# Attention in-projection as three fp32r products per block, and expert outputs added to token rows in DRAM by an accumulating indirect DMA

## What is computed

```python
def moba_mixer(h, pos, k_past, v_past, w_in, w_out):
    proj = (h @ w_in).astype(jnp.float32)
    q, k, v = jnp.split(proj, [nqd, nqd + nkd], axis=-1)
    ...
def moe_swiglu(h, w_router, w_gate, w_up, w_down):
    logits = (h @ w_router).astype(jnp.float32)
    top_val, top_idx = lax.top_k(logits, TOP_K)
    wts = jax.nn.softmax(top_val, axis=-1)
    gates = jnp.sum(jax.nn.one_hot(top_idx, N_EXPERTS) * wts[..., None], axis=-2)
    y = jnp.zeros(h.shape, jnp.float32)
    for e in range(N_EXPERTS):
        y = y + gates[..., e:e + 1] * swiglu(h, w_gate[e], w_up[e], w_down[e])
    return y
```

## Time and profile before

| | us |
|---|---|
| runs of the kernel before | 1921.21, 1921.53, 1923.94 (median 1921.53) |
| the profiled execution, its own time | 1925.23 |
| its span from first to last instruction | 1923.0 |
| TensorE busy | 1779.1 (93%) |
| VectorE busy | 1293.0 (67%) |
| ScalarE busy | 968.4 (50%) |
| in-projection of attention | 606 to 675 |
| K and V pages read | 678 to 832 |
| router and gather of the first expert | 873 to 909 |
| experts | 909 to 1897 |

### The profile page before, as it was taken

How to read it: one execution, slowest core, us unless ns; L and a number is a source line. 1 busy time by engine, 2 the same in 40 slices (tenths; PEclk the granted TensorE clock), 3 DMA queues, 4 the chain that set the end, 5 groups by cost and what they waited for, 6 DMA issues and landing times.

```text
span 1923.0 us, 26967 instructions
## 1 busy us (share of the span) xinstructions
PE 1779.1 (93%) x9794; PEld 1483.7 (77%) x9794; DVE 1293.0 (67%) x1399; ACT 968.4 (50%) x908; POOL 53.3 (3%) x82
## 2 busy tenths in 40 slices
PE   5999988899999973896999999999999999999996
PEld 4888886899997731365888888888888888888885
DVE  5864573555543241014888888988889888888885
ACT  3442230444431030002777777776777777777773
POOL 1240000000000000000000000000000000000000
PEclk9998798999999996885999999999999999999998
DMA  7322123355546699972899999999999999999991
GB/s 291 110 80 103 48 118 154 138 190 177 178 157 238 201 325 386 346 300 89 317 363 384 346 370 362 345 382 350 365 365 334 387 352 362 371 348 358 357 351 57
DMA packets 98893, 521.85 MB, mean 271 GB/s; under 512 B 11066, under 2 KB 11259, under 8 KB 46067
## 3 DMA queue, kind: packets, MB, share of 16 engines
q1 hardware_dynamic: 82592, 482.72, 66.8%
q10 hardware_dynamic: 13970, 25.46, 3.7%
q0 software_dynamic: 2240, 12.49, 1.8%
HBM read 512.30 MB, written 8.33 MB: 271 GB/s over the span
## 4 chain that ended last, share of the span: by engine, by line
PE 78%; issue 9%; DVE 7%; ACT 2%; ACTq 2%; DMA 1%; SPq 1%; POOLq 0%; POOL 0%; DVEq 0%
PE bank L994 14%; PE bank L996 14%; PE bank L995 14%; PE bank L503 6%; PE bank L504 5%; PE bank L505 5%; PE bank L744 3%; PE bank L810 3%; PE bank L911 1%; PE bank L615 1%; PE bank L988 1%; PE bank L1033 1%; ACTq L408 1%; PE bank L660 1%; DVE ring L1625 1%
## 5 line engine op out<-in xcount | busy, mean ns | idle before, releaser
L1829 DVE TENSOR_TENSOR w_lo<-raw_w,w_hi 128x2048 fp32r<-128x2048 f32 x336 | 768.8, 2290 | 120.7 <-ACT w_hi L1276 116.4
L1276 ACT ACTIVATE w_hi<-raw_w 128x2048 fp32r<-128x2048 f32 x336 | 644.8, 1920 | 362.4 <-PE bank L996 273.5
L994 PE MATMUL bank<-w_hi,xe_hi 128*128 128x512 f32 x896 | 364.9, 407 | 1.5 <-DVE xe_lo L1890 1.5
L996 PE MATMUL bank<-w_hi,xe_lo 128*128 128x512 f32 x896 | 350.1, 391 | 0.0
L995 PE MATMUL bank<-w_lo,xe_hi 128*128 128x512 f32 x896 | 349.5, 390 | 0.0
L504 PE MATMUL bank<-fh_lo,w_hi 128*128 128x264 f32 x704 | 202.3, 287 | 0.0
L996 PEld LDWEIGHTS bank<-w_hi,xe_lo 128*128 128x128 f32 x896 | 168.6, 188 | 36.0
L994 PEld LDWEIGHTS bank<-w_hi,xe_hi 128*128 128x128 f32 x896 | 168.7, 188 | 35.8 <-issue 1.8
L995 PEld LDWEIGHTS bank<-w_lo,xe_hi 128*128 128x128 f32 x896 | 168.8, 188 | 33.8
L994 PE MATMUL bank<-w_hi,aT_hi 128*128 128x512 f32 x448 | 176.7, 394 | 0.0
L996 PE MATMUL bank<-w_hi,aT_lo 128*128 128x512 f32 x448 | 174.7, 390 | 0.0
(11 more groups left out here) (340 smaller groups left out, 2204.7 us busy)
## 6 DMA issues: line engine op xcount, KB each, us to landing
raw_w<-in_moe SPq DMA_DIRECT2D x336, 1024.0 KB, 5.6
raw_w<-in_ffn_w SPq DMA_DIRECT2D x42, 1024.0 KB, 4.8
ring<-in_k_pages SPq DMA_DIRECT2D x96, 256.0 KB, 3.5
raw_w<-in_gdn_in SPq DMA_DIRECT2D x16, 1024.0 KB, 5.2
ring<-in_v_pages SPq DMA_DIRECT2D x64, 256.0 KB, 11.7
ring<-in_v_pages ACTq DMA_DIRECT2D x64, 256.0 KB, 11.6
ring<-in_att_in SPq DMA_DIRECT2D x4, 2048.0 KB, 7.7
ring<-in_k_pages ACTq DMA_DIRECT2D x32, 256.0 KB, 7.7
```

Source lines behind the costliest of these rows:

```text
L994: mm(out, hi, move_hi, start=first, stop=False)
L996: return mm(out, lo, move_hi, start=False, stop=last)
L1276: A(w_hi[:, p % SPLIT, :], raw_w[:, p % RAW, :], ACT.Copy).then_inc(split_hi, 1)
L1829: V.tensor_tensor(w_lo[:, p % SPLIT, :], raw_w[:, p % RAW, :], w_hi[:, p % SPLIT, :].bitcast(F32), ALU.subtract).then_inc(split_lo, 1)
```

## The change

In attention, a half block of weights (128x512) becomes a unit: ScalarE copies it from `ring` to one of four buffers `a_units` (in the memory of `f_lo`) in fp32r, VectorE puts the remainder beside it, and each of the 128 fp32 products becomes three fp32r ones with `fh_hi` and `fh_lo`. `slot_free` waits for a chunk's eight remainders in place of its four blocks. The input's parts are made within `norm(2)`, as in the dense layer's norm: ScalarE copies the high part of each tile when it is normed, VectorE makes the remainder of tile k - 2 behind tile k (`rest_of_input`). `rope` and `rot_t` lie elsewhere in `scr`.

In the experts `pick_g`, `spread` and `combine` go. `number_slots` gives, by the same product with a second column, each slot's gate too; empty slots get rows of their own behind the tokens' (each DRAM tensor has T + 128 rows, cleared by POOL from a zeroed `ye`). ScalarE scales `ye` by the slot's gate as it copies, and POOL adds its 128 rows to `y_dram` by an accumulating indirect DMA (`add_rows`), in its stream behind the fetch for the next expert. VectorE keeps that expert's row numbers and gates in `slot_put` and `gate_put` from piece 12 on. Behind the last expert POOL loads the sums back to `htok`, and TensorE transposes them (`turn_sums`) for the eight additions.

`slot_free`:

```diff
             elif m < C_K:
-                eng.wait_ge(aproj, 4 * (m - C_AIN + 1))
+                eng.wait_ge(split_lo, FFN_PIECES + 8 * (m - C_AIN + 1))
```

TensorE:

```diff
             for c in range(16):
-                if c % 4 == 0:
-                    arrived(C_AIN + c // 4)
                 for k in range(KT):
+                    n = 2 * c + k // 4
+                    if k % 4 == 0:
+                        pe.wait_ge(split_lo, FFN_PIECES + n + 1)
                     if c == 0:
-                        pe.wait_ge(normed, 2 * KT + k + 1)
-                    last = mm(bank[c % 4][:, 0:T], tile4(C_AIN + c // 4)[:, c % 4, k, :], hT[:, k, :],
-                              start=(k == 0), stop=(k == KT - 1))
+                        pe.wait_ge(fh_lo_set, 2 * KT + k + 1)
+                    hi, lo = (a_units[:, n % ATT_UNITS, i, P * (k % 4):P * (k % 4 + 1)] for i in range(2))
+                    last = stationary_mm(bank[c % 4][:, 0:T], hi, lo, fh_hi[:, k, :], fh_lo[:, k, :], k == 0, k == KT - 1)
...
-                    last = mm(bank[0][:, 0:1], pick[:, i, :], tok_no[:, i:i + 1], start=(i == 0), stop=(i == 2))
+                    last = mm(bank[0][:, 0:2], pick[:, i, :], tok_gate[:, i, :], start=(i == 0), stop=(i == 2))
...
-            def combine(v, d):
-                if d == 0:
-                    pe.wait_ge(ye_sb, v * 2 + 2)
+            def turn_sums(d):
                 if d >= 2:
-                    pe.wait_ge(comb_added, v * KT + (d - 1))
-                mm(bank[4 + d % 2][:, 0:T], ye[:, P * d:P * (d + 1)], spread, start=True, stop=True).then_inc(comb, 1)
+                    pe.wait_ge(comb_added, d - 1)
+                for i, (t0, n) in enumerate(TOK_TILES):
+                    last = nc.tensor.transpose(bank[4 + d % 2][:, t0:t0 + n], htok[0:n, i, P * d:P * (d + 1)], ident[0:n, 0:n])
+                last.then_inc(comb, 1)
...
-                    if not first and 5 <= p < 5 + 2 * KT and p % 2 == 1:
-                        combine(v - 1, (p - 5) // 2)
...
             gather(0)
+            number_slots(0)
```

ScalarE:

```diff
+            def split_a(n):
+                c = n // 2
+                if n == 0:
+                    act.wait_ge(f_used, PIECES)
+                if n >= ATT_UNITS:
+                    act.wait_ge(aproj, c - 1)
+                if n % 8 == 0:
+                    act.wait_ge(ring_full[(C_AIN + c // 4) % SLOTS], full_value(C_AIN + c // 4))
+                A(a_units[:, n % ATT_UNITS, 0, :], att_half(n), ACT.Copy).then_inc(split_hi, 1)
...
             def take_y(v):
                 act.wait_ge(piece_used, v * PIECES + PIECES)
+                act.wait_ge(put_set, v + 1)
+                act.wait_ge(y_rows, v * 16 + Y_CLEAR)
                 for half in range(2):
-                    A(ye[:, N * half:N * (half + 1)], bank[4 + half][:, :], ACT.Copy).then_inc(ye_sb, 1)
+                    A(ye[:, N * half:N * (half + 1)], bank[4 + half][:, :], ACT.Copy, scale=gate_put).then_inc(ye_sb, 1)
```

POOL:

```diff
+            def add_rows(v):
+                pool.wait_ge(put_set, v + 1)
+                pool.wait_ge(ye_sb, 2 * v + 2)
+                G.indirect_dma_start(y_dram, bass.IndirectOffsetOnAxis(ap=slot_put[:, 0:1], axis=0), ye, None,
+                                     compute_op=ALU.add).then_inc(y_rows, 16)
+            def sums_back(experts):
+                pool.wait_ge(gathered, 2 * experts + 2)
+                pool.wait_ge(y_rows, Y_CLEAR + 16 * experts)
+                for i, (t0, n) in enumerate(TOK_TILES):
+                    pool.dma_start(htok[0:n, i, :], y_dram[t0:t0 + n, :]).then_inc(tok_rows, 16)
```

VectorE:

```diff
             def expert(v, first=False):
                 for p in range(PIECES):
...
-                    if not first and 9 <= p < 9 + 2 * KT and p % 2 == 1:
-                        add_combined(v - 1, (p - 9) // 2)
+                    if p == 12:
+                        if not first:
+                            dve.wait_ge(y_rows, v * 16 + Y_CLEAR)
+                        V.tensor_copy(gate_put, gate_tok)
+                        V.tensor_copy(slot_put[:, :], slot_tok[:, :]).then_inc(put_set, 1)
...
             pick_tokens(0)
+            slots(0)
+            dve.wait_ge(slot_set, 1)
             rest_of_gathered(0)
```

More of the change, by code:

```diff
@@ L1013, in expert @@
                     else:
-                        if p == UP_PIECES:
-                            pe.wait_ge(spread_sb, v + 1)
+                        if p == UP_PIECES and not first:
+                            pe.wait_ge(ye_sb, v * 2)
                         for i in range(F_PIECE):
@@ L1035, in expert @@
                         last.then_inc(act_turned, 1)
-                    if p == 24:
-                        if not first:
-                            pe.wait_ge(comb_added, v * KT)
-                        for i, (t0, n) in enumerate(TOK_TILES):
-                            last = nc.tensor.transpose(bank[4][0:CAP, t0:t0 + n], pick_g[0:n, i, :], ident[0:n, 0:n])
-                        last.then_inc(spread_ps, 1)
                     if p == 32:
@@ L1226, in _ @@
                 A(aq[:, c, :], bank[c % 4][:, 0:T], ACT.Copy).then_inc(aproj_sb, 1)
+                for n in range(2 * c + ATT_UNITS, min(2 * c + ATT_UNITS + 2, 32)):
+                    split_a(n)
             for t in range(CH):
@@ L1730, in _, with rest_of_att, turn_heads @@
                 square_x(d - 1, f_added, d)
-            norm(2)
-            dve.wait_ge(prm_loaded, 64)
-            for c in range(12):
+            def rest_of_att(n):
+                dve.wait_ge(split_hi, FFN_PIECES + n + 1)
+                V.tensor_tensor(a_units[:, n % ATT_UNITS, 1, :], att_half(n), a_units[:, n % ATT_UNITS, 0, :].bitcast(F32),
+                                ALU.subtract).then_inc(split_lo, 1)
+            for n in range(2):
+                rest_of_att(n)
+            norm(2, lambda k: rest_of_input(k - 2, 2) if k >= 2 else None)
+            rest_of_input(KT - 2, 2)
+            rest_of_input(KT - 1, 2)
+            for n in range(2, ATT_UNITS):
+                rest_of_att(n)
+            def turn_heads(c):
                 a = aq[0:ROT, c, :]
                 dve.wait_ge(rot_ps, c + 1)
+                if c == 0:
+                    dve.wait_ge(prm_loaded, 64)
                 if c >= 1:
@@ L1741, in _ @@
                 V.tensor_tensor(a, a, rot_t[0:ROT, :], ALU.add).then_inc(roped, 1)
+            for c in range(16):
+                for n in range(2 * c + ATT_UNITS, min(2 * c + ATT_UNITS + 2, 32)):
+                    rest_of_att(n)
+                if 1 <= c <= 12:
+                    turn_heads(c - 1)
             dve.wait_ge(roped, 12)
@@ L1923, in expert @@
                     if p == 34:
-                        dve.wait_ge(slot_ps, v + 1)
-                        V.tensor_copy(slot_tok[:, :], bank[0][:, 0:1]).then_inc(slot_set, 1)
+                        slots(v + 1)
                     if p == PIECES - 1:
```

111 lines of the change are left out of this document (72 added, 39 removed).

## The result

| | before | after |
|---|---|---|
| runs beside each other, median (us) | 1921.37 (1918.53 to 1923.94, 4 runs) | 1898.88 (1896.15 to 1902.26, 4 runs) |
| ratio, 95% interval | | 0.9884 [0.9862, 0.9906] |
| the same kernels in a later session | 1920.12 (11 runs) | 1899.91 (1897.41 to 1907.65, 6 runs); 0.9899 [0.9883, 0.9915] |
| profiled execution, span | 1923.0 | 1896.1 |
| TensorE, VectorE, ScalarE busy | 1779.1, 1293.0, 968.4 | 1734.7, 1288.5, 985.2 |

The account below looks back on a forecast made before the run. TensorE was taken as the bound, carrying 78% of the chain that ended last. Terms -10.7 - 0.5 + 0.5 - 28.2 + 12.0 = -26.9, off the median of 1921.53, gave 1894.6 us; range 1885 to 1907.

Parts of the forecast that it names:

- In-projection: Attention's in-projection: 24 fp32r products at 0.1213 replace eight fp32 ones per block, 2.91 against 3.76; -10.7 us, bounds -5 to -11.6.
- 12 rotations of 0.56: In-projection's block phase: rotations priced at 0.56 each, beside 14 blocks of 2.91, 47.5 us together.
- K pages: Attention's page reading: SP no longer waits for in-projection blocks, so the page phase moves earlier as a whole; -0.5 us more.
- Router to first expert: Between router and first expert: VectorE saves 0.9, but slot numbers made before the first expert add 1.4; +0.5 us.
- Experts: Expert loop: TensorE loses eight combining products of 0.45 and the gates' turning of 0.37 per expert; -28.2 us, bounds -22 to -29.
- The end: After the last product: add to DRAM, loading of sums and transposes come before the first addition; +12 us, bounds +7 and +20.
- Rival 1: Experts: the weight stream becomes the bound, an add taking 2.7 us of queues; 1922.8 in full, 1908.7 half; chance 0.08.
- Rival 2: Experts: adds land after VectorE's wait before piece 13, costing 7 times the excess over 28 us; 1991 or more; chance 0.04.
- Rival 3: In-projection: split halves come late from VectorE's fixed order, each block losing 0.5; 1900 us; chance 0.05.
- Rival 4: In-projection: TensorE saves time but page reading ends no earlier, transfers being the limit; price 11, 1905.8 us; chance 0.06.

Follow-up runs that it names:

- the last experiment: Changed kernel with sums of experts 0 to 6 read during expert 7, in-projection touched up, first expert's remainders ahead of its slot numbers: 1881.40 us, ratio 0.9789 to before.

## Why the prediction was right, and where it was off

The time, 1898.88, lies in the range, 4.3 above the forecast, and the side was right. By its steps:

- *In-projection, -10.7, measured -7.5 by the two traces (-5.3 to -7.7 by the other kernels with this in-projection).* The mechanism was right, the products' price of 0.1213 too. Two terms were too small. "12 rotations of 0.56" is the rotation's row in the chain, and another 0.2 of its cost stood in the 3.76 of the block behind it, which the prediction took for a plain block's price: 12 x 0.19 = 2.3. It could have been read in the earlier trace rows, where 10.89 for the last three blocks makes at most 3.63 for one without a rotation. And the first rotation came 0.9 later behind the dense layer's end than forecast: the reciprocal 0.4, through ScalarE's two copies and the table's load, as moving the load shows; the first block 0.7, 7.5 from the reciprocal's end and not 6.84, with a clock of 0.54 to the end of it, where the dense layer's likeness ran its last products at 0.12; less 0.25, by which the rope table landed faster (4.56).
- *K pages, -0.5.* SP has indeed no wait left between 600 and 700, and issues without a pause, as its timeline shows (start, duration, line):

```profile
595.50 103.79 SPq L423 DMA_DIRECT2D ring<-in_k_pages  x90
```

  Nothing more came of it: the first product with V pages comes at the same distance from the last block as before.
- *Router to first expert, +0.5, measured 0.0*: gather 1.7 earlier relative to the router's first product (18.0 against 19.7; 18.0 to 19.1 in the other kernels with the new experts), first product 1.7 later behind it. Slots ahead of the first expert cost as forecast, and the last experiment took 1.4 back.
- *Experts, -28.2, measured -31.* Per expert 4.4 instead of 3.97. The mechanism was right and the instructions' prices a little low: from start to start the combining products gave 3.7 and not 3.6, the turning of the gates 0.56 and not 0.37, and a group of transposes behind it another 0.14.
- *The end, +12, measured +15.4.* The order of steps was right. The add was taken as the gather's low end plus one, 7, and came at 6.9; the issue came at 2.1, not 1.3; the sums took 5.7 from the first issue to TensorE's start, where three issues and the 3.4 of a store made 4.6; the transposes and additions ran at 0.82 instead of 0.69 a tile, since TensorE's clock had fallen to the 1.2 GHz level. By the estimate from the Trainium skill ("DMA: Bandwidth & Descriptors", the anatomy of one DMA) the add would take 3.2 and the sums 4.5, +7 in all. The trace has 6.4 and 5.7, so it is further off than the rows were.
- *Rival 1* was right in its price per add (2.7) and wrong in the place of the bound, which lies 9 us of queue time per expert beyond the change. *Rival 2* was right in its place and its 28 us; its price is 0.7 and not 1 per microsecond. *Rival 3* did not come: the halves were ready in time, and a block's extra time was its rotation's. *Rival 4* fell.

By stretches the misses are +3.2 in the in-projection, +2.8 up to the gather (the V stage began 0.7 later behind the last block and took 0.7 longer, the output projection took 1.6 longer at a lower clock, and the gather came 1.7 sooner after the router's start), +0.3, -2.8 in the experts and +3.4 at the end, 6.9 in all. That the two profiles differ by the forecast's 26.9 hid them, by luck: between these the dense layer, which the change doesn't touch, happened to end 6.9 earlier. Without that, -26.9 + 6.9 = -20.0, which is what the larger set of runs gives (-20.2).

## What to carry to other kernels

An add to DRAM that lands after 11 us is free inside a loop that has 28 us of cover for it; the round trip costs its full length at the loop's end, where nothing is left to hide it: keep the last turn on the old path and read the rest of the sums one turn early. A DMA share near 1 beside a fully busy engine doesn't say that the stream is the bound; add known transfers and see when the first microsecond comes through. And price an instruction by stretches with it and without it, from start to start: the rotation's own row said 0.56, and its neighbours carried another 0.2. Look also at what the new work of an engine pushes behind it, a table's load for instance.

## What the runs showed that I had not expected

- A rotation (weights of 128 rows by 32 columns) between products with weights of 128 by 128 costs TensorE 0.75 to 0.76, 0.3 more than its two records of 0.22, between plain fp32 products and between fp32r ones alike, and in pairs the 0.3 is paid half as often. A plain fp32 product with weights of 128 by 128 between fp32r ones costs only its own two records: 0.45 for a norm sum, 0.46 for a combining product.
- With the same in-projection code, one block behind the wait for the rope table ran at a granted clock of 0.72 in three of eight profiles and took 5.2 instead of 3.66; the output projection took 40.3 to 43.3 as the clock at its start was 0.97 to 0.55.
- An accumulating indirect DMA of 128 rows of 4 KB takes 2.6 to 2.7 us of all 16 queues beside about 1.3 for a plain one of the same count of packets and bytes, and lands after 6.4 alone and 11.1 beside the weights; plain, 3.5 and 9.5.
- SP issues page loads one per 1.15 us even where nothing makes it wait: 90 in 103.79.
